# Two transformer blocks on one core: the first block's weight casts and remainders moved ahead of the convolution's taps, with four neighbouring steps

## The chip, the core and the metric

The kernel runs on one core of a Trainium2 chip, written by hand for its five engines: TensorE (PE in the rows; PEld is its weight load), VectorE (DVE), ScalarE (ACT), GpSimd (POOL) and SyncE (SP), which issues the weights' DMAs. Engines meet through semaphores only. The metric is the device time of one execution in microseconds (us).

## What is computed

Two blocks follow each other on 256 tokens of width 1024, batch 1, float32. The change lies in the mixing part of the first block, which reduces to this:

```python
h = rms_norm(x, pre_mix_norm)
proj = h @ w_in                          # att q, k, v | gdn qkv | z | a, b
o_att = softmax attention, 8 heads of 64, with relative bias
qkv = silu(causal_conv(gdn_qkv, 4 taps)) # 1536 channels
g = -exp(A_log) * softplus(a + dt_bias)  # per token and head
g_cum = cumsum(g) within chunks of 64
decay = exp(where(causal, g_cum_i - g_cum_j, -inf))
m = strict_lower(k_beta k^T * decay)     # then (I + m) is solved for u and w
o_gdn = the gated recurrence over the chunks, with q k^T * decay
x = x + rms_norm([o_att, o_gdn] @ w_out)
```

The MLP of the first block and the whole second block come behind it and are untouched.

## The kernel before, in words

Every product in float32 is made from rounded halves: a weight tile `raw` (128 x 2048) is cast to `wh` on ScalarE (function `hi`, L1152) and its remainder `raw - wh` is put into `wl` on VectorE (function `lo`, L1649). TensorE then adds three products per tile. A tile is a *unit*; units are numbered in the order of a list, PLAN, and each engine walks that list. Units 0 to 5 are the convolution's inputs (query, key and value channels, two channel groups each), 6 and 7 the gate z, 8 and 9 the attention's keys (called `qk` 0 and 1), 10 and 11 its queries (`qk` 2 and 3), 12 and 13 its values.

`raw` has 3 slots and `wh` and `wl` have 4. SyncE loads unit i into its slot when `lo(i - 3)` is done; `hi(i)` waits for the load and for TensorE to have finished unit i - 4; `lo(i)` waits for `hi(i)`; TensorE waits for `lo(i)`. On ScalarE and VectorE the call `next_unit()` issues all casts or remainders up to two units ahead of the engine's own count (AHEAD is 2).

Every engine runs its instructions in the order in which they are written. The order around the change is this.

On TensorE: units 0 to 3, the sums of the decays (L684, L685, and L689, whose result is `grow`), units 4 and 5, the two units of z (L506), the sums of squares (L658), unit 8, the turned sums `rn` and the token-major values and keys (`tm`, `kd`, transposes at L417), unit 9, then the products of keys and queries `KQ` (L752, eight banks in four pairs), units 10 and 11, and L764, which waits for VectorE's `spread`. A product goes to one of eight PSUM banks, and TensorE waits until the bank's last reader is done. Unit 4 goes to the bank of unit 2, whose reader is the scaling `cin` 2 on VectorE. The banks of `KQ` 2 and 3 were those of the second `tm` tile and of `kd`; the bank of `KQ` 5 was that of unit 9.

On VectorE, a loop over u = 0 to 5: scale the unit's output into `cin` (L1670), `next_unit()`, then six tap instructions (L1678) that add the taps 1 to 3 to the tap 0 that ScalarE has made. For u = 3 it also copies the cumulated decays (`gcum`) and prepares `kdx`, which frees a bank that z uses. For u = 5 there are eight of the sixteen differences of `dU` before the taps and eight after the loop (`differences`, one instruction for each of 16 pairs of chunk pair and head). Then come `keys(0)`, a scaling of unit 8's output that waits for that unit; the norms up to `bk`; the product of `dU` with `bk` (`db`); `kdx` and `kd`; the remainders of units 10 and 11; `keys(1)`, which waits for unit 9; a loop over the eight `KQ` banks; and, without another wait for TensorE, the steps up to `spread` (L1670).

On ScalarE, the loop over u casts ahead, makes the taps 0 (L1290) and, for u = 3, copies `grow` out of PSUM, sends it to DRAM, runs three `silu` instructions, waits for that DMA and reads the rows back, spread over all partitions, into `dU`. Behind the loop it casts units 8 and 9, then makes the squares (L1269) that TensorE's sums of squares need.

Of the kernel before, what the change touches and what calls it, by code (L numbers as in the profile page):

```python
# [189 lines left out]
def rep(a, m):  # L190
    return a.unsqueeze(1).broadcast_to([128, m, a.shape[1]])
# [10 lines left out]
def halves(a):  # L202
    return a.rearrange("p (a s) -> p a s", a=2)
# [162 lines left out]
def build(nc, A, out):  # L366
    with ExitStack() as top:
# [15 lines left out]
        def par(name):  # L383
            a, w = SM[name]
            return M.small[:, a:a + w]
# [752 lines left out]
        def scalar(e):  # L1138
# [4 lines left out]
            def hi(upto):  # L1143

                while done[0] < min(upto + 1, len(PLAN)):
                    i = done[0]
                    done[0] += 1
                    r, h = i % RR, i % HR
                    q.wait_dma(raw_in[r], 16 * (i // RR + 1))
                    if i >= HR:  # L1150
                        q.wait_ge(PE, ("unit", i - HR))
                    e.copy(M.wh[:, h, :], M.raw[:, r, :]).then_inc(q.sem, q.tick(("hi", i)))  # L1152

            def next_unit():
                hi(unit[0] + AHEAD)
                unit[0] += 1
# [102 lines left out]
            def silu_of(u):  # L1259
                q.wait_ge(DV, ("tap", 2 * u + 1, 3))  # L1260
                o = M.cout[:, 2 * u:2 * u + 2, :]
                e.activation(o, o, ACT.Silu).then_inc(q.sem, q.tick(("silu", u)))
# [9 lines left out]

            for u in range(6):
                next_unit()
                if u == 0:
                    q.wait_ge(DV, "sn0")
                    e.activation(M.sn, M.sn, ACT.Exp).then_inc(q.sem, q.tick("sn1"))
                    q.wait_ge(DV, "eb")
                    e.activation(M.eb1, M.eb1, ACT.Exp, scale=-1.0).then_inc(q.sem, q.tick("eb1"))
                    q.wait_dma(LD["small"])  # L1280
                    e.activation(M.ea, par("A_log"), ACT.Exp).then_inc(q.sem, q.tick("ea"))
                    q.wait_ge(q, "sn1")
                    e.activation(M.sn, M.sn, ACT.Ln, bias=1.0).then_inc(q.sem, q.tick("sn2"))
                if u == 4:
                    silu_of(3)
                q.wait_ge(DV, ("cin", u))
                q.wait_ge(PO, "pad")
                for i in range(2):
                    a = 2 * u + i
                    e.activation(M.cout[:, a, :], M.cin[:, a, 0:S], ACT.Copy,  # L1290
                                 scale=cw[:, a, 0:1]).then_inc(q.sem, q.tick(("tap", a, 0)))
                if u == 3:
                    q.wait_ge(PE, "grow")
                    e.copy(M.grow, bank[at["grow"]][0:16, 0:128]).then_inc(q.sem, q.tick("grow"))
                    q.wait_ge(q, "grow")
                    e.dma_start(A["gscr"], M.grow).then_inc(LD["gscr"], 16)
                    silu_of(0)
                    silu_of(1)
                    silu_of(2)
                    q.wait_dma(LD["gscr"])  # L1300
                    e.dma_start(M.dU[:], bass.AP(A["gscr"].tensor, 0, [[0, 128], [128, 16], [1, 128]])).then_inc(
                        LD["dU"], 16)
                elif u == 5:
                    silu_of(4)
# [331 lines left out]
        def vector(e):  # L1636
# [4 lines left out]
            def lo(upto):  # L1641

                while done[0] < min(upto + 1, len(PLAN)):
                    i = done[0]
                    done[0] += 1
                    r, h = i % RR, i % HR
                    q.wait_dma(raw_in[r], 16 * (i // RR + 1))
                    q.wait_ge(AC, ("hi", i))
                    e.tensor_tensor(M.wl[:, h, :], M.raw[:, r, :], M.wh[:, h, :].bitcast(F32),  # L1649
                                    ALU.subtract).then_inc(q.sem, q.tick(("lo", i)))  # L1650

            def next_unit():
                lo(unit[0] + AHEAD)
                unit[0] += 1
# [14 lines left out]
            def tt(o, a, b, op, *names):  # L1669
                return e.tensor_tensor(o, a, b, op).then_inc(q.sem, q.tick(*names))  # L1670

            def ts(o, a, s1, s2, op0, op1, *names):
                if op1 is None:
                    return e.tensor_scalar(o, a, s1, None, op0).then_inc(q.sem, q.tick(*names))
                return e.tensor_scalar(o, a, s1, s2, op0, op1).then_inc(q.sem, q.tick(*names))

            def stt(o, a, s, b, op0, op1, *names):
                return e.scalar_tensor_tensor(out=o, in0=a, scalar=s, in1=b, op0=op0,  # L1678
                                              op1=op1).then_inc(q.sem, q.tick(*names))
# [98 lines left out]
            def scaled(u):  # L1778
                q.wait_ge(PE, ("conv", u))
                q.wait_ge(AC, "rbc")  # L1780
                tt(M.cin[:, 2 * u:2 * u + 2, 3:], halves(bank[at["conv", u]][:]), rep(M.rbc, 2), ALU.mult, ("cin", u))
# [8 lines left out]
            def differences(lo_, hi_):  # L1790
                q.wait_dma(LD["dU"])
                for s in range(lo_, hi_):
                    stt(M.dU[:, s, :], M.dU[:, s, :], M.gcum[:, s:s + 1], M.cap, ALU.subtract, ALU.min, "dU")

            for u in range(6):
                if u:
                    scaled(u)
                if u < 5:
                    next_unit()
                if u == 0:  # L1800
                    q.wait_ge(AC, "eb1")
                    ts(M.eb1, M.eb1, 1.0, None, ALU.add, None, "eb2")
                    q.wait_ge(q, "eb2")
                    e.reciprocal(M.beta, M.eb1).then_inc(q.sem, q.tick("beta"))
                    q.wait_ge(AC, "sn2")
                    stt(M.sn, M.sa1, 0.0, M.sn, ALU.max, ALU.add, "sn3")
                    q.wait_ge(q, "sn3")
                    q.wait_ge(AC, "ea")
                    stt(M.graw.rearrange("p (c h) -> p c h", c=2), M.sn.rearrange("p (c h) -> p c h", c=2), -1.0,
                        rep(M.ea, 2), ALU.mult, ALU.mult, "graw")  # L1810
                elif u == 5:
                    next_unit()
                    differences(0, 8)
                    next_unit()
                for k in range(1, 4):
                    for i in range(2):
                        a = 2 * u + i
                        q.wait_ge(AC if k == 1 else q, ("tap", a, k - 1))
                        stt(M.cout[:, a, :], M.cin[:, a, k:k + S], cw[:, a, k:k + 1], M.cout[:, a, :], ALU.mult,
                            ALU.add, ("tap", a, k))  # L1820
                if u == 3:
                    q.wait_ge(PE, "sums")
                    b = at["sums"]
                    e.tensor_copy(M.gcum, bank[b][:, 0:16]).then_inc(q.sem, q.tick("gc"))
                    q.wait_ge(q, "gc")
                    tt(M.kdx, bank[b][:, 16:32], M.gcum, ALU.subtract, "kdx0")

            differences(8, 16)
            next_unit()

            def keys(u):

                q.wait_ge(PE, ("qk", u))
                tt(M.kTa[:, 2 * u:2 * u + 2, :], halves(bank[at["qk", u]][:]), rep(M.rbc, 2), ALU.mult, ("qk", u))
# [11 lines left out]
            e.reciprocal(bk, rk).then_inc(q.sem, q.tick("bk0"))  # L1846
            q.wait_ge(q, "bk0")
            tt(M.bk, M.bk, M.beta, ALU.mult, "bk")
            q.wait_ge(AC, "dexp")
            q.wait_ge(q, "bk")  # L1850
            tt(M.dU[:], M.dU[:], bc(M.bk, 128), ALU.mult, "db")
# [3 lines left out]
            q.wait_ge(PE, "kd")  # L1855
            tt(heads(M.kd), heads(bank[at["kd"]][:]), bc(M.kdx[:, 0:8], 64), ALU.mult, "kd")
            next_unit()
            next_unit()
            keys(1)

            def att_scores(h):
                nm = gs[:, 192 + 4 * (h % 4):194 + 4 * (h % 4)]
# [590 lines left out]
        for engine in (tensor, scalar, vector, gpsimd):  # L2453
            engine(Counting())
# [4 lines left out]
        block.sync(sync)  # L2459
        block.gpsimd(gpsimd)  # L2460
        block.scalar(scalar)
        block.vector(vector)
        block.tensor(tensor)

# [48 lines left out]
```

## Time and profile before

| | |
|---|---|
| median of 3 runs | 901.58 us (900.99 to 903.89) |
| the profiled execution's own time | 901.5 us |
| its span, first to last instruction | 899.3 us |
| mean granted TensorE clock | 0.997 of full speed |

The span and the own time belong to one execution; the 2.2 us between them lie outside the program's instructions. Times in the rows further down are us from the start of the span.

### The profile page before, as it was taken

The page shows a single profiled execution, that of the slowest core. Times are in us where ns is not written, and L with a number is a line of the kernel's source. Part 1 is how long each engine was busy: PE and PEld are TensorE (multiplying, and loading weights), DVE is VectorE, ACT ScalarE, POOL GpSimd, SP SyncE. Part 2 cuts the span into 40 slices and gives each one's busy share as a digit, 9 for nine tenths or more (in the row PEclk, how much of TensorE's full clock was granted, in tenths as well). Part 3 has the DMA queues.
Part 4 walks back from the last instruction along what each step waited for, and adds up shares of the span by engine and source line. Part 5 has one row for each costly group of instructions (what it writes and reads, how often), then busy time and mean ns, then how long its engine had stood idle before and what let it go on. Part 6 is the DMA issues. An engine that isn't in the chain of part 4 may idle for free.

```text
span 899.3 us, 12704 instructions
## 1 busy us (share of the span) xinstructions
PE 886.7 (99%) x5404; PEld 758.7 (84%) x5404; DVE 608.4 (68%) x734; ACT 455.8 (51%) x550; POOL 82.6 (9%) x93
## 2 busy tenths in 40 slices
PE   9999999999999999999999999999999999999997
PEld 8889788788888887888888888888888888888885
DVE  5989886776556657778858665766557566664655
ACT  6683563654445446555443355443355555444543
POOL 1001230100000000000124210110100000000000
PEclk9999999999999999999999999999999999999999
DMA  9675315156555553654564544354554356455531
GB/s 329 257 253 185 101 59 201 48 175 257 195 193 187 188 187 140 223 188 156 206 220 168 187 166 162 141 187 187 187 187 147 155 190 234 176 180 206 187 141 47
DMA packets 26264, 161.51 MB, mean 180 GB/s; under 512 B 3608, under 2 KB 4280, under 8 KB 8288
## 3 DMA queue, kind: packets, MB, share of 16 engines
q1 hardware_dynamic: 23616, 153.40, 46.7%
q0 software_dynamic: 2272, 6.24, 2.0%
q10 hardware_dynamic: 320, 1.06, 0.3%
q8 instruction: 42, 0.69, 0.3%
q14 instruction: 14, 0.11, 0.0%
HBM read 159.62 MB, written 2.64 MB: 180 GB/s over the span
## 4 chain that ended last, share of the span: by engine, by line
PE 79%; DVE 13%; ACT 3%; DMA 2%; issue 2%; SPq 1%; POOL 0%; POOLq 0%; ACTq 0%; DVEq 0%
PE banks L506 34%; PE banks L474 21%; PE banks L477 10%; DVE t_wl L1649 5%; PE banks L578 3%; PE banks L534 2%; PE banks L417 1%; DMA t_x<-in_x 1%; PE banks L775 1%; ACT t_wh L1152 1%; DVE t_xt L1670 1%; PE banks L980 1%; PE banks L1114 1%; DVE t_cout L1678 1%; PE banks L429 1%
## 5 line engine op out<-in xcount | busy, mean ns | idle before, releaser
L1649 DVE TENSOR_TENSOR t_wl<-t_raw,t_wh 128x2048 fp32r<-128x2048 f32 x136 | 312.2, 2317 | 111.2 <-ACT t_wh L1152 110.1
L474 PE MATMUL banks<-t_hx,t_wh 128*128 128x512 f32 x992 | 312.0, 396 | 0.0
L1152 ACT CAST t_wh<-t_raw 128x2048 fp32r<-128x2048 f32 x136 | 255.8, 1906 | 15.9 <-DMA t_raw<-in_W 9.4
L477 PEld LDWEIGHTS banks<-t_hx,t_wl 128*128 128x128 f32 x992 | 186.3, 188 | 43.7
L477 PE MATMUL banks<-t_hx,t_wl 128*128 128x256 f32 x992 | 194.9, 278 | 0.0
L474 PEld LDWEIGHTS banks<-t_hx,t_wh 128*128 128x128 f32 x992 | 153.4, 189 | 2.4
L506 PE MATMUL banks<-t_wh,t_hx 128*128 128x512 f32 x320 | 101.7, 394 | 0.2 <-DVE t_wl L1649 0.2
L506 PEld LDWEIGHTS banks<-t_wh,t_hx 128*128 128x128 f32 x320 | 59.5, 188 | 13.0 <-DVE t_wl L1649 0.4
L506 PE MATMUL banks<-t_wl,t_hx 128*128 128x512 f32 x160 | 61.1, 390 | 0.0
L2297 POOL TENSOR_TENSOR t_st<-t_st,t_half 128x1 f32<-128x1 f32 (+1 forms) x18 | 10.6, 589 | 433.6 <-DVE t_st L1678 425.7
L1487 ACT COPY t_hold<-banks 128x512 f32<-128x512 f32 x28 | 16.4, 584 | 65.3 <-PE banks L477 54.7
L429 PE MATMUL banks<-t_hx,t_wh 128*128 128x256 f32 x192 | 36.5, 292 | 1.9 <-DVE t_wl L1649 1.9
L1446 ACT COPY t_tail<-banks 128x512 f32<-128x512 f32 x14 | 8.2, 586 | 54.8 <-PE banks L477 54.8
L506 PEld LDWEIGHTS banks<-t_wl,t_hx 128*128 128x128 f32 x160 | 30.1, 188 | 6.1
L506 PE MATMUL banks<-t_wh,t_mh 128*128 128x512 f32 x112 | 34.6, 390 | 0.0
L506 PE MATMUL banks<-t_wl,t_mh 128*128 128x512 f32 x112 | 34.5, 389 | 0.0
L506 PE MATMUL banks<-t_wh,t_ml 128*128 128x512 f32 x112 | 34.5, 389 | 0.0
L429 PEld LDWEIGHTS banks<-t_hx,t_wh 128*128 128x128 f32 x192 | 31.0, 199 | 2.9 <-DVE t_wl L1649 2.2
L1670 DVE TENSOR_TENSOR t_rl<-banks,t_tail 128x512 f32<-128x512 f32 x14 | 9.7, 691 | 28.0 <-ACT t_tail L1446 28.0
L429 PE MATMUL banks<-t_hx,t_wl 128*128 128x256 f32 x96 | 27.8, 290 | 0.0
L2397 POOL TENSOR_SCALAR t_gt<-t_gt,t_small 128x256 f32<-128x256 f32 x16 | 14.6, 926 | 117.6 <-ACT t_gt L1556 117.6
L1613 ACT COPY t_gtail<-banks 128x512 f32<-128x512 f32 x11 | 6.4, 586 | 37.4 <-PE banks L477 37.4
(335 smaller groups left out, 1322.3 us busy)
## 6 DMA issues: line engine op xcount, KB each, us to landing
t_raw<-in_W SPq DMA_DIRECT2D x139, 1024.0 KB, 4.8
t_raw<-in_W SPq DMA_DIRECT2D x8, 256.0 KB, 6.3
t_raw<-in_W SPq DMA_DIRECT2D x4, 512.0 KB, 9.1
skew<-scr POOLq DMA_DIRECT2D x1, 1536.0 KB, 14.4
t_cout<-in_xT SPq DMA_DIRECT2D x4, 256.0 KB, 5.3
t_x<-in_x SPq DMA_DIRECT2D x2, 512.0 KB, 10.8
t_dU<-gscr ACTq DMA_DIRECT2D x1, 1024.0 KB, 7.5
t_tab<-in_tab POOLq DMA_DIRECT2D x1, 640.0 KB, 7.6
```

Source lines behind the costliest of these rows:

```text
L429: m = e.matmul(bank[b][:, c * S:c * S + S], W[w][:, h, k * 256 + c * 128:k * 256 + c * 128 + 128], H[a][:, k, :], start=k == 0 and n == 0, ...
L474: e.matmul(bank[b + c], M.wh[:, h, wk], M.hx[:, k, :, :].rearrange("p a s -> p (a s)"), start=k == 0, stop=False)
L477: m = e.matmul(bank[b + c][:, 0:S], M.wl[:, h, wk], M.hh[:, k, :], start=False, stop=k == 7)
L506: m = e.matmul(bank[outs[t][c]][:], act[a][:, ks[kk], t * 128:t * 128 + 128], W[w][:, h, kk * 512 * ncb + c * 512:kk * 512 * ncb + c * 512 ...
L534: m = e.matmul(bank[outs[t][c]][:], act[a][:, k, t * 128:t * 128 + 128], W[w][:, (i0 + u) % HR, kk * 1024 + c * 512:kk * 1024 + c * 512 + ...
L578: m = e.matmul(bank[bo][:], H[a][:, k, t * 128:t * 128 + 128], W[w][:, (i0 + k // 4) % HR, (k % 4) * 512:(k % 4) * 512 + 512], start=k == ...
L1152: e.copy(M.wh[:, h, :], M.raw[:, r, :]).then_inc(q.sem, q.tick(("hi", i)))
L1487: e.copy(halves(M.rest[:, s, :]), both(M.banks, at[tile], 1)).then_inc(q.sem, q.tick((tile, "rest")))
L1649: e.tensor_tensor(M.wl[:, h, :], M.raw[:, r, :], M.wh[:, h, :].bitcast(F32), ALU.subtract).then_inc(q.sem, q.tick(("lo", i)))
L1670: return e.tensor_tensor(o, a, b, op).then_inc(q.sem, q.tick(*names))
L2297: return e.tensor_tensor(o, a, b, op).then_inc(q.sem, q.tick(*names))
L2397: e.tensor_scalar(M.gt[:, a, :], M.gt[:, a, :], gw[:, 4 * h + a:4 * h + a + 1], None, ALU.mult).then_inc(q.sem, q.tick(("gt", h, a)))
```

## The change

Four edits, all in the order of instructions; no instruction is added or removed.

1. In the loop over u, ScalarE casts and VectorE subtracts one unit further ahead, before the taps of step u: unit 4 at u = 1, unit 5 at u = 2, unit 6 at u = 3, and units 7 and 8 before the taps of u = 4. ScalarE's cast of unit 7 stands behind the taps of u = 3.
2. ScalarE copies `grow` and sends it to DRAM at u = 2. The three `silu`, the wait for that DMA and the read into `dU` stay at u = 3, behind the cast of unit 7.
3. VectorE makes the 16 differences together, behind the loop and behind the remainder of unit 9 (before, that remainder stood behind them).
4. VectorE makes the remainder of unit 10 and then `keys(1)` right behind `bk`, ahead of `db`, `kdx` and `kd`; the remainder of unit 11 stays behind `kd`.

```diff
 # scalar
             for u in range(6):
                 next_unit()
+                hi(min(u + 3, 6) if u < 4 else 8)
...
-                if u == 3:
+                if u == 2:
                     q.wait_ge(PE, "grow")
                     e.copy(M.grow, bank[at["grow"]][0:16, 0:128]).then_inc(q.sem, q.tick("grow"))
                     q.wait_ge(q, "grow")
                     e.dma_start(A["gscr"], M.grow).then_inc(LD["gscr"], 16)
+                elif u == 3:
+                    hi(7)
                     silu_of(0)
                     silu_of(1)
                     silu_of(2)
 # vector
                 if u < 5:
                     next_unit()
+                    lo(u + 3 if u < 4 else 8)
...
                 elif u == 5:
                     next_unit()
-                    differences(0, 8)
                     next_unit()
...
-            differences(8, 16)
+            lo(9)
+            differences(0, 16)
             next_unit()
...
             tt(M.bk, M.bk, M.beta, ALU.mult, "bk")
+            next_unit()
+            keys(1)
             q.wait_ge(AC, "dexp")
             q.wait_ge(q, "bk")
             tt(M.dU[:], M.dU[:], bc(M.bk, 128), ALU.mult, "db")
...
             tt(heads(M.kd), heads(bank[at["kd"]][:]), bc(M.kdx[:, 0:8], 64), ALU.mult, "kd")
             next_unit()
-            next_unit()
-            keys(1)
```

## Rows read from the trace of the kernel before

**Rows 1.** The page, part 1: busy time, share of the span, instructions.

```profile
PE 886.7 (99%) x5404; PEld 758.7 (84%) x5404; DVE 608.4 (68%) x734; ACT 455.8 (51%) x550; POOL 82.6 (9%) x93
```

**Rows 2.** TensorE's waits over the span: us in total, times, longest.

```profile
PE banks L429 <- DVE t_wl L1649: 1.9, 1, 1.9
...
PE banks L619 <- POOL t_st L2297: 0.6, 1, 0.6
```

**Rows 3.** The chain that ended last, 30 to 100 us: start, length, what.

```profile
40.67 4.67 DMA gscr<-t_va
...
45.74 1.92 ACT t_wh L1152
...
50.10 11.18 PE banks L506 x48
...
62.28 5.95 PE banks L429 x48
...
90.34 1.24 DVE t_cin L1670
...
91.62 1.99 PE banks L764 x4
```

**Rows 4.** Timeline of TensorE: start, us, line, operation, tiles, [idle before <-releaser].

```profile
34.34 0.39 PE L689 MATMUL banks<-t_tab,t_gs 128*16 128x128 f32 x2
36.63 0.79 PE L429 MATMUL banks<-t_hx,t_wh 128*128 128x256 f32 x2 [1.90 <-DVE t_wl L1649]
...
62.21 0.51 PE L429 MATMUL banks<-t_hx,t_wh 128*128 128x256 f32 x2
...
75.66 2.00 PE L752 MATMUL banks<-t_cout 64*128 64x256 f32 x16
77.89 2.00 PE L752 MATMUL banks<-t_cout 64*128 64x256 f32 x16 [0.23 <-DVE t_kTa L1670]
```

**Rows 5.** Two stretches: us, busy us by engine, granted clock, DMA share, GB/s.

```profile
20.00:36.60 16.60, 14.09 (x112) 12.91 (x110) 13.32 (x32) 10.99 (x19) 3.30 (x5) 1.00 0.71 276
36.65:40.05 3.40, 3.40 (x16) 3.40 (x17) 3.40 (x8) 0.92 (x3) 0.00 (x0) 0.50 0.64 228
```

**Rows 6.** Timeline of VectorE, 30 to 78 us.

```profile
30.04 0.68 DVE L1670 TENSOR_TENSOR t_cin<-banks,t_rbc 128x512 f32<-128x512 f32 x1
...
33.68 0.69 DVE L1670 TENSOR_TENSOR t_cin<-banks,t_rbc 128x512 f32<-128x512 f32 x1
34.28 2.29 DVE L1649 TENSOR_TENSOR t_wl<-t_raw,t_wh 128x2048 fp32r<-128x2048 f32 x1
36.48 2.46 DVE L1678 SCALAR_TENSOR_TENSOR t_cout<-t_cin,t_small,t_cout 128x256 f32<-128x256 f32 x6
...
61.81 2.19 DVE L1678 SCALAR_TENSOR_TENSOR t_dU<-t_dU,t_gs,t_tab 128x128 f32<-128x128 f32 x8
...
69.73 2.29 DVE L1670 TENSOR_TENSOR t_dU<-t_dU,t_gs 128x2048 f32<-128x2048 f32 x1
...
72.14 0.69 DVE L1670 TENSOR_TENSOR t_tm<-banks,t_gs 128x512 f32<-128x512 f32 x1
...
77.15 0.69 DVE L1670 TENSOR_TENSOR t_kTa<-banks,t_rbc 128x512 f32<-128x512 f32 x1
77.75 0.41 DVE L1678 SCALAR_TENSOR_TENSOR t_hold<-banks,t_dU 128x256 f32<-128x256 f32 x1
```

**Rows 7.** Timeline of ScalarE, 41 to 61 us.

```profile
41.03 1.28 ACT L1262 ACT_TABLE_LOAD   x1 [0.39 <-ACT t_va L1294]
42.32 1.68 ACT L1262 ACTIVATE t_cout<-t_cout 128x512 f32<-128x512 f32 x3
...
53.06 0.91 ACT L1290 ACTIVATE t_cout<-t_cin,t_small 128x256 f32<-128x256 f32 x2 [2.28 <-DVE t_cin L1670]
...
58.51 2.00 ACT L1269 ACTIVATE t_cin<-t_cout 128x1024 f32<-128x1024 f32 x2
```

**Rows 8.** DMA issues between 36.5 and 36.8 us: size, us to landing.

```profile
t_raw<-in_W SPq DMA_DIRECT2D x1, 1024.0 KB, 8.9
```

## The prediction

> **What bounds the kernel now.** I read the busy shares first. TensorE is busy for 99% of the span [rows 1], so a gain has to come from the few places where TensorE waits, or runs at half its clock. Then TensorE's waits: the only long one is 1.9 us for unit 4's remainder [rows 2]; behind it the granted clock stands at 0.50 for 3.4 us, that is at 1.2 of 2.4 GHz, after 1.00 before [rows 5]. The reader should not book those 1.9 us and the lost clock as the gain, for the chain that ended last says what really sets the pace next: the decays' rows go to DRAM at 40.67 and take 4.67 us, ScalarE can't pass the wait for them and casts unit 6 only at 45.74, and so z starts at 50.10 [rows 3]. TensorE's late unit 4 was hidden behind that. The next place on the chain is `spread`: it ends at 90.34 + 1.24 = 91.58, and TensorE's L764, which waits for it, starts at 91.62 [rows 3]. From the first instruction of the loop over the `KQ` banks, at 77.75, VectorE needs 13.83 us to that end [rows 3, 6], and nothing in the loop or behind it waits for TensorE, whose `KQ` is written by then. So the sum needs two times in the new order: when TensorE reaches z and unit 8, and when VectorE reaches the `KQ` loop.
>
> **The casts one step ahead.** Steps on VectorE, from start to start: a scaling takes 0.60 us (33.68 to 34.28), a remainder 2.20 (34.28 to 36.48), six taps 2.46 less the 0.09 by which neighbours overlap, 2.37 [rows 6]. The order up to the scaling at 30.04 is untouched. From there: unit 4's remainder at 30.64, the taps of u = 1 at 32.84, the scaling of u = 2 at 35.21, ending at 35.89. The remainder is ready 3.7 us sooner, but unit 4 on TensorE wants the PSUM bank that this scaling reads out, so it starts at about 35.95 and not at 34.73, where the sums end (34.34 + 0.39), nor at 36.63 as before [rows 4]. The gap shrinks from 1.90 to 1.2 us. Does the clock still fall? A wait of 0.6 us left it at 1.00, one of 1.90 didn't [rows 2, 5]; 1.2 us lies half way. I take it that it holds, because the shortened gap leaves 0.7 us of matmuls in the place of idleness, and keep the fall for a rival.
>
> Units 4 and 5 at full clock take about 5.9 us each (5.95 for a unit with its last matmul, [rows 3]), together 11.8 with the overlap: TensorE is ready for z at 47.75. z needs unit 6's remainder (VectorE: scaling of u = 3 at 40.4, remainder 41.0 to 43.2) and the bank that the sums of the decays left (read by 45.9). ScalarE's cast of unit 6 now stands before the silu and ends by 39.3. Nothing is late, and z starts 2.35 us sooner.
>
> **The decays' rows.** `grow` is copied by 37 instead of 40.6; its DMA lands at 41.7 by the 4.67 of [rows 3]. ScalarE has by then: taps of u = 3 to 42.0, cast of unit 7 to 43.9 (its load is issued 3.7 us sooner too, and with the 8.9 us of [rows 8] lands at 41.8), table load 1.28 and three silu 1.68 [rows 7], so the read into `dU` is issued at 46.9, behind 45.4 before, without a wait. At 8.9 us, the slowest load of that size here, it lands at 55.8. The differences start at 59.9, so its delay costs nothing. SyncE's queue only gains: each load waits for a remainder, and those come sooner.
>
> **ScalarE becomes the next limit.** Cast of unit 8 to 49.2 (1.92 us a cast, [rows 3]); VectorE's remainder of unit 8 waits 0.4 us for it and ends at 51.4; taps, then the last scaling ends at 54.4. Then ScalarE makes its last taps (0.91), one silu (0.56), the cast of unit 9 (1.92) and the squares (2.00) [rows 3, 7], which end at 59.7. TensorE ends z at 47.75 + 11.18 = 58.9 [rows 3], and the second half of the sums of squares waits for those squares: unit 8 starts at 60.2 against 62.21 [rows 4]. The lead is 2.0 us.
>
> **The differences together.** Sixteen take 2 x 2.19 less an overlap, 4.3 us [rows 6]; with unit 9's remainder ahead of them they run from 59.9 to 64.2, against an end at 64.0 before. ScalarE's exponential and cast of unit 10 follow by 68.2 and VectorE's remainder of unit 10 by 70.4. All this lies beside TensorE's units 8 and 9. Without that cover, each 0.1 us would be paid.
>
> **The second keys' scaling.** This is where the lead goes. TensorE's work from unit 8's start to `KQ` is 75.66 - 62.21 = 13.45 us [rows 4], so `KQ` starts at 73.65, and `keys(1)`, which needs the last matmul of unit 9, can't start before 73.75. VectorE reaches it at 70.4 and stands still for 3.35 us with `db`, `kdx`, `kd`, unit 11's remainder and the `KQ` loop queued behind it. Before, `db` to `kd` and most of both remainders ran while TensorE made unit 9. Now, from 73.75: `keys(1)` 0.60, `db` with `kdx` 2.41 (69.73 to 72.14), `kd` 0.60, remainder 2.20 [rows 6]. The loop starts at 79.56 against 77.75, 1.8 us late in spite of the lead of 2.0. What the edit buys is the 0.23 us that TensorE waited for `keys(1)` at 77.89 [rows 4].
>
> TensorE meets it too: the third bank pair's partner in `KQ` 2 and 3 is read by `kd`, which ends at 73.75 + 0.60 + 2.41 + 0.69 = 77.45. After the first pair (1.0 of 2.00 us) TensorE idles from 74.7 to 77.5. From there it needs 1.0 and then what it needed between 77.89 and 91.6, 13.7 us [rows 3, 4]: it is ready for L764 at 92.2, and `spread` comes at 91.58 + 1.81 = 93.4. So L764 is 1.8 us late. But a gap of 2.8 us is longer than the one behind which the clock fell; 3.4 us at half clock [rows 5] cost up to 1.7, which uses up the 1.2 us of slack and puts L764 at up to 93.9. I take 93.6: plus 2.0 us. Bounds: plus 1.8 without the fall, plus 2.3 with all of it. TensorE and VectorE both stand behind `spread`, and I see no slack that gives the time back.
>
> The Trainium skill has two places that bear on this. "TensorE: Matmul & The Clock Gate", in "Architectural detail", says that ScalarE and VectorE queues are strictly first in, first out. By this rule `db` can't pass the waiting `keys(1)`; if it could, the lead would carry through and the time be 899.5. The same page's table under "Why this matters for your kernels" lets a gap longer than 1.90 us pass before the clock falls; by it neither gap costs any and the time is 903.3. This trace shows a fall behind 1.90 us, and the measurement decides.
>
> **The sum.** The profiled execution took 901.5 us, 2.2 more than its span; it is 0.1 under the median of 901.58, so I take it for the median. 901.5 + 2.0 = 903.5.
>
> **The rivals.**
> First, the clock falls in the first gap as well. It decides if 1.2 us of idleness behind the small matmuls of the sums are enough. Units 4 and 5 then take up to 1.7 us more, z ends at 60.6, its squares are no longer waited for, and unit 8 starts at 61.6 instead of 60.2. Everything behind is 1.4 later: 904.9, slower by 0.4%. For it: 1.90 us were enough. Against: 0.6 were not. Page "TensorE: Matmul & The Clock Gate", "What's actually happening", of the Trainium skill says that the monitor doesn't start over with a kernel, so the same gap may do it in one run and not in the next; no row here shows it.
> Second, the hold doesn't bind: unit 9 is done when VectorE asks, and the lead of 2.0 stays, 899.5. That needs unit 9 to end at 70.4, 3.3 us sooner than TensorE's own work allows; or else VectorE's other work turns out short. Little speaks for it.
> Third, nothing is seen: the lateness at `spread` is taken up in the next stage, where short steps pass between three engines, 901.5. For it: SyncE and ScalarE have slack there. Against: TensorE and VectorE are late together.
>
> **How the numbers follow.** Forecast, 903.3 to 903.9: 0.55. First rival 0.20, second 0.10, third 0.15. About 0.3%, 2.7 us, is what a measurement of this kernel can tell from no change; slower thus begins at 904.3. Slower: most of the first rival and the forecast's upper tail, 0.28. Faster, under 898.9: part of the second, 0.06. Same: 0.66. The range reaches from 900.0, between the second and the third rival, to 905.4, over the first.
>
> **What would show it.** Right: unit 4 waits about 1.2 us for `cin`, with the clock at 1.00 behind it; z starts near 47.8; unit 8 near 60.2; VectorE idles over 3 us before the second scaling of keys; TensorE idles 2 to 3 us inside `KQ`, for `kd`; L764 starts near 93.5. Wrong: another transfer or cast that stops ScalarE between 42 and 58, no idle time before `keys(1)`, or an L764 that is no later than 91.6.

## The result, and the profile after

The changed kernel takes 903.66 us (median of 10 runs, 903.17 to 904.57) against 901.25 us of the kernel before (10 runs beside it). The ratio is 1.0026, with a 95% interval of 1.0016 to 1.0036: 2.4 us slower, a loss that the interval tells from nothing, and one of the size that was forecast (2.0 us).

The profiled execution of the changed kernel has a span of 902.5 us, 3.2 more than that of before. Not all of this belongs to the change: VectorE's scaling of u = 1, ahead of everything that was moved, starts at 30.80 instead of 30.04 [rows 6], because `x` was loaded later (ScalarE's first work on it starts at 19.66 instead of 18.91). Where absolute times of two traces are compared below, such a shift is taken off (0.76 us here), which puts both on the scale of before. What is left is 2.1 us from L764 on, and still 2.1 us at L1114 in the second block (712.81 against 709.98). About 0.35 us more appear only behind it, where nothing was changed and where this execution has a wait of 0.21 us that the other lacks; I count them as chance. So the traces show a loss of 2.1 us, the medians one of 2.4 us with an interval of 1.4 to 3.2.

TensorE's waits in the changed kernel, over the span:

```profile
PE banks L752 <- DVE t_tm L1673: 2.8, 1, 2.8
PE banks L429 <- DVE t_cin L1673: 1.3, 1, 1.3
...
PE banks L658 <- ACT t_cin L1269: 0.6, 2, 0.3
```

The wait of 1.9 us for unit 4's remainder [rows 2] is one of 1.3 us for the scaling of u = 2, and a new wait stands above it: 2.8 us inside `KQ`, for the tile that `kd` writes. TensorE's timeline shows where:

```profile
36.81 0.36 PE L429 MATMUL banks<-t_hx,t_wh 128*128 128x256 f32 x1 [1.31 <-DVE t_cin L1673]
...
48.40 0.40 PE L506 MATMUL banks<-t_wh,t_hx 128*128 128x512 f32 x1
...
61.26 0.50 PE L429 MATMUL banks<-t_hx,t_wh 128*128 128x256 f32 x2
...
74.69 1.13 PE L752 MATMUL banks<-t_cout 64*128 64x256 f32 x8
78.64 4.31 PE L752 MATMUL banks<-t_cout 64*128 64x256 f32 x24 [2.82 <-DVE t_tm L1673]
...
94.50 0.68 PE L764 MATMUL banks<-t_cin,t_tab 128*128 128x512 f32 x1
```

z (L506) starts directly behind unit 5 at 48.40, or 47.64 on the scale of before, where 47.75 was worked out. Unit 8 starts at 61.26, or 60.5 on the scale of before, against 62.21 [rows 4]: the lead is there, 1.7 us. `KQ` starts at 74.69, and 4 us later TensorE is still at its first quarter. L764 starts 2.88 us later than in [rows 3], 2.12 with the shifted start taken off. VectorE's timeline has the reason:

```profile
69.39 2.29 DVE L1652 TENSOR_TENSOR t_wl<-t_raw,t_wh 128x2048 fp32r<-128x2048 f32 x1 [0.74 <-ACT t_wh L1152]
74.79 0.69 DVE L1673 TENSOR_TENSOR t_kTa<-banks,t_rbc 128x512 f32<-128x512 f32 x1 [3.11 <-PE banks L429]
75.40 2.28 DVE L1673 TENSOR_TENSOR t_dU<-t_dU,t_gs 128x2048 f32<-128x2048 f32 x1
...
77.80 0.69 DVE L1673 TENSOR_TENSOR t_tm<-banks,t_gs 128x512 f32<-128x512 f32 x1
78.41 2.28 DVE L1652 TENSOR_TENSOR t_wl<-t_raw,t_wh 128x2048 fp32r<-128x2048 f32 x1
80.61 0.42 DVE L1681 SCALAR_TENSOR_TENSOR t_hold<-banks,t_dU 128x256 f32<-128x256 f32 x1
...
93.20 1.22 DVE L1673 TENSOR_TENSOR t_cin<-t_kb,t_tab 128x1024 f32<-128x1024 f32 x1
```

The reader should follow VectorE's queue: the remainder of unit 10 ends at 71.68, then nothing for 3.11 us, because the scaling of the second keys (first row with `t_kTa`) waits for TensorE's unit 9. Only then come `db`, `kdx` and `kd`, which in [rows 6] ran from 69.73 on, while TensorE still made that unit. The `KQ` loop starts at 80.61 instead of 77.75, `spread` ends at 94.42 instead of 91.58. That is the loss, 2.1 us on the common scale.

The long gap also cost TensorE its clock, while the gap ahead of unit 4 did not, as three stretches show (us, busy us of PE, PEld, DVE, ACT and POOL, granted clock, DMA share, GB/s):

```profile
36.90:48.00 11.10, 11.10 (x93) 11.10 (x94) 11.06 (x19) 8.43 (x11) 0.00 (x0) 1.00 0.86 326
...
78.25:81.55 3.30, 2.91 (x14) 2.60 (x16) 3.30 (x5) 0.00 (x0) 0.00 (x0) 0.50 0.00 0
81.65:94.50 12.85, 12.85 (x109) 12.45 (x107) 12.68 (x22) 2.40 (x2) 1.03 (x2) 1.00 0.47 164
```

`KQ` runs on at 1.2 GHz, half the clock. It matters little: TensorE ends unit 11 just when `spread` ends, so the fall used up TensorE's slack and added less than 0.1 us.

On ScalarE one thing went otherwise than forecast:

```profile
42.62 0.34 ACTq L1304 DMA_DIRECT2D t_dU<-gscr  x1
42.69 1.89 ACT L1152 CAST t_wh<-t_raw 128x2048 fp32r<-128x2048 f32 x1
44.60 1.28 ACT L1262 ACT_TABLE_LOAD   x1
45.89 1.68 ACT L1262 ACTIVATE t_cout<-t_cout 128x512 f32<-128x512 f32 x3
48.18 1.92 ACT L1152 CAST t_wh<-t_raw 128x2048 fp32r<-128x2048 f32 x1 [0.61 <-DMA t_raw<-in_W]
```

The read into `dU` (ACTq) is written behind the cast of unit 7 and the three silu, yet it is issued at 42.62, ahead of them: as soon as the DMA of the decays' rows that it waits for had landed (issued at 37.78, 4.8 us to landing). So the sentence that every engine runs its instructions in the order in which they are written does not hold for a DMA that ScalarE's program issues. The cast of unit 8 then waits 0.61 us for its load.

### The profile page after: what moved, and what is told of

Its sections match the earlier page's. It is cut to its first block, busy times and chain, and to the rows that moved or that the text cites. A ratio compares the mean times of both kernels' runs of the same rounds, so it can differ in the third digit from the quotient of the medians.

```text
span 902.5 us, 12704 instructions
## 1 busy us (share of the span) xinstructions
PE 886.7 (98%) x5404; PEld 758.4 (84%) x5404; DVE 608.0 (67%) x734; ACT 455.6 (50%) x550; POOL 83.7 (9%) x93
## 4 chain that ended last, share of the span: by engine, by line
PE 77%; DVE 13%; ACT 5%; DMA 2%; issue 2%; SPq 1%; POOL 0%; POOLq 0%; DVEq 0%; ACTq 0%
PE banks L506 32%; PE banks L474 19%; PE banks L477 10%; DVE t_wl L1652 6%; PE banks L429 3%; PE banks L578 3%; PE banks L534 2%; ACT t_wh L1152 2%; PE banks L417 1%; DMA t_x<-in_x 1%; PE banks L775 1%; DMA t_raw<-in_W 1%; PE banks L980 1%; DVE t_cout L1681 1%; DVE t_cv L1681 1%
## 5 line engine op out<-in xcount | busy, mean ns | idle before, releaser
L506 PE MATMUL banks<-t_wh,t_hx 128*128 128x512 f32 x320 | 101.6, 394 | 0.0
L506 PEld LDWEIGHTS banks<-t_wh,t_hx 128*128 128x128 f32 x320 | 59.5, 188 | 12.5 <-issue 0.3
L506 PE MATMUL banks<-t_wl,t_hx 128*128 128x512 f32 x160 | 61.1, 390 | 0.0
L506 PEld LDWEIGHTS banks<-t_wl,t_hx 128*128 128x128 f32 x160 | 30.1, 188 | 6.1
L506 PE MATMUL banks<-t_wh,t_mh 128*128 128x512 f32 x112 | 34.6, 390 | 0.0
L506 PE MATMUL banks<-t_wl,t_mh 128*128 128x512 f32 x112 | 34.5, 389 | 0.0
L506 PE MATMUL banks<-t_wh,t_ml 128*128 128x512 f32 x112 | 34.5, 389 | 0.0
## 6 DMA issues: line engine op xcount, KB each, us to landing
t_dU<-gscr ACTq DMA_DIRECT2D x1, 1024.0 KB, 11.6
```

The lines of the kernel that those rows point to most:

```text
L506: m = e.matmul(bank[outs[t][c]][:], act[a][:, ks[kk], t * 128:t * 128 + 128], W[w][:, h, kk * 512 * ncb + c * 512:kk * 512 * ncb + c * 512 ...
```

## The experiments

The comparisons are with the kernel before, run on the same chip beside each group. Kernels that build on others are named by what they change. Where the times of two runs are subtracted, the medians are; the ratio compares each run with the kernel before beside it.

**Is it the second keys?** First the fourth edit undone, then that edit alone.

```diff
             tt(M.bk, M.bk, M.beta, ALU.mult, "bk")
-            next_unit()
-            keys(1)
...
             next_unit()
+            next_unit()
+            keys(1)
```

> The changed kernel with the fourth edit undone (remainder of unit 10 and second keys' scaling back behind the decays' product and kd). If the hold of VectorE at the second keys' scaling is the whole loss: VectorE makes the decays' product, kd and both remainders while TensorE makes unit 9, no wait of over 1 us before that scaling, TensorE's wait inside KQ at most 1 us, and spread 1.2 us sooner than in the kernel before: 900.1, ratio 0.9985. If the casts one step ahead are themselves what costs (loads that collide, ScalarE held up): still about 903.5, ratio 1.0025.

Measured: 899.5 us, ratio 0.9979 (0.9970 to 0.9987). VectorE's timeline of this run:

```profile
67.20 2.29 DVE L1673 TENSOR_TENSOR t_dU<-t_dU,t_gs 128x2048 f32<-128x2048 f32 x1
69.41 0.17 DVE L1673 TENSOR_TENSOR t_gs<-t_gs 128x16 f32<-128x16 f32 x1
69.61 0.69 DVE L1673 TENSOR_TENSOR t_tm<-banks,t_gs 128x512 f32<-128x512 f32 x1
70.22 4.48 DVE L1652 TENSOR_TENSOR t_wl<-t_raw,t_wh 128x2048 fp32r<-128x2048 f32 x2
74.62 0.68 DVE L1673 TENSOR_TENSOR t_kTa<-banks,t_rbc 128x512 f32<-128x512 f32 x1
75.22 0.41 DVE L1681 SCALAR_TENSOR_TENSOR t_hold<-banks,t_dU 128x256 f32<-128x256 f32 x1
```

No row has idle time before it: the same instructions fill the time of unit 9, and the loop starts at 75.22, or 75.91 on the scale of before, 1.8 us sooner than there. `spread` is 1.9 us sooner, where 1.2 was expected. Three of the four edits make the kernel 2.1 us faster; the fourth turns that into a loss of 2.4.

> The kernel before with the fourth edit alone. If the hold is the loss, it costs more here, where there is no lead of 2 us to pay for it: the KQ loop starts 3.8 us later than in the kernel before, L764 3.8 to 4.3 us later, 905.1 to 905.6, ratio 1.0043 to 1.0048, and TensorE waits about 2.8 us for kd inside KQ. If the loss comes from the casts: no change, or the 0.2 us that TensorE waited for the second keys.

The edit is the other half of the diff, put into the kernel before. Measured: 905.66 us, ratio 1.0047 (1.0035 to 1.0060). Alone the fourth edit costs 4.1 us, as was worked out. TensorE's waits:

```profile
PE banks L752 <- DVE t_tm L1670: 2.8, 1, 2.8
PE banks L506 <- DVE t_wl L1649: 2.1, 2, 1.8
```

The second row bears on the reading of the kernel before. In this run the clock stood at 1.00 behind the gap of 1.88 us ahead of unit 4. Its stretch, and then the start of z in this run and in the kernel before (both traces are on the same scale):

```profile
36.65:40.05 3.40, 3.40 (x28) 3.40 (x29) 3.40 (x8) 0.92 (x3) 0.00 (x0) 1.00 0.61 234
...
50.20 0.50 PE L506 MATMUL banks<-t_wh,t_hx 128*128 128x512 f32 x1 [1.79 <-DVE t_wl L1649]
...
50.10 0.50 PE L506 MATMUL banks<-t_wh,t_hx 128*128 128x512 f32 x1 [0.19 <-DVE t_wl L1649]
```

TensorE was ready for z at 48.41, 1.5 us sooner than the 49.91 of the kernel before, and stood 1.8 us waiting for unit 6's remainder. z started at 50.20, with the fallen clock at 50.10. So the lost clock ahead of unit 4 was indeed hidden: in this stage TensorE could be later by nearly those 1.8 us without z being later.

**Does TensorE's wait for `kd` count by itself?**

```diff
             tt(M.bk, M.bk, M.beta, ALU.mult, "bk")
-            next_unit()
-            keys(1)
-            q.wait_ge(AC, "dexp")
             q.wait_ge(q, "bk")
-            tt(M.dU[:], M.dU[:], bc(M.bk, 128), ALU.mult, "db")
...
             tt(heads(M.kd), heads(bank[at["kd"]][:]), bc(M.kdx[:, 0:8], 64), ALU.mult, "kd")
             next_unit()
+            keys(1)
+            q.wait_ge(AC, "dexp")
+            tt(M.dU[:], M.dU[:], bc(M.bk, 128), ALU.mult, "db")
+            next_unit()
```

> The changed kernel with kdx and kd ahead of the remainder of unit 10 and the second keys' scaling; the decays' product and the remainder of unit 11 stay behind it. TensorE's bank is then free when it reaches KQ 2 and 3. If VectorE's lateness sets the end and TensorE's wait for kd adds only what the fallen clock costs: spread 0.6 to 0.8 us sooner than in the changed kernel, 902.5 to 902.8, ratio 1.0014 to 1.0017. If TensorE's wait of 2.8 us for kd is the cause by itself: 2 us sooner or more, about 901, ratio 1.000.

Measured: 902.7 us, ratio 1.0013 (1.0004 to 1.0022). TensorE no longer waits inside `KQ`; it waits behind it, for the first bank that the late loop frees:

```profile
PE banks L429 <- DVE t_dU L1673: 2.2, 1, 2.2
```

The clock stood at 0.50 there too (80.00 to 83.30). The loop starts 0.9 us sooner than in the changed kernel on the scale of before, which is about the time of `kdx` and `kd` on VectorE, and the median is 1.0 us lower. So TensorE's wait for `kd` is not the cause by itself: without it VectorE's lateness remains, and TensorE idles for that at another place.

**Can the hold be filled the other way round?** `db`, `kdx`, `kd` and unit 10's remainder before the second keys, the loop right behind them, unit 11's remainder behind the loop and unit 12's behind `spread`.

```diff
             tt(M.bk, M.bk, M.beta, ALU.mult, "bk")
-            next_unit()
-            keys(1)
...
             tt(heads(M.kd), heads(bank[at["kd"]][:]), bc(M.kdx[:, 0:8], 64), ALU.mult, "kd")
             next_unit()
+            keys(1)
...
                ALU.mult, "spread")
             next_unit()
+            next_unit()
```

> The changed kernel, with the decays' product, kdx, kd and the remainder of unit 10 before the second keys' scaling, the KQ loop right behind it, the remainder of unit 11 behind the loop, and that of unit 12 behind spread. If the hold is the loss and the lead of 2 us is real: VectorE waits under 1 us for unit 9, the loop starts at about 74.4 on the scale of the kernel before, TensorE is the later of the two at L764 and keeps the lead: 899.3, ratio 0.998. If the next stage takes all leads back: 901.3, ratio 1.000.

Measured: 900.61 us, ratio 0.9987 (0.9978 to 0.9996): faster than before, but 1.1 us behind the plain order, and not what was forecast. TensorE's waits, and below them three rows of VectorE's timeline, say why:

```profile
PE banks L775 <- DVE t_xt L1673: 1.3, 1, 1.3
PE banks L429 <- DVE t_cin L1673: 1.3, 1, 1.3
...
74.32 0.69 DVE L1673 TENSOR_TENSOR t_kTa<-banks,t_rbc 128x512 f32<-128x512 f32 x1 [0.74 <-PE banks L429]
75.38 0.42 DVE L1681 SCALAR_TENSOR_TENSOR t_hold<-banks,t_dU 128x256 f32<-128x256 f32 x1 [0.36 <-PE banks L752]
...
89.11 4.49 DVE L1652 TENSOR_TENSOR t_wl<-t_raw,t_wh 128x2048 fp32r<-128x2048 f32 x2
```

L764 no longer waits for `spread`, but two remainders now stand between `spread` and a later product of VectorE that TensorE needs (`t_xt`, L775). VectorE had idled 0.74 us for the second keys and 0.36 us ahead of the loop, together the 1.1 us that are missing. With the plain order it is idle for only 0.40 us between the first keys' scaling and that product. My reading is that VectorE has next to no time to spare there: putting off work moves the wait, and an idle moment is lost.

**What limits the lead?** The next four take the run with the fourth edit undone as their base, or, the last of them, the kernel before.

```diff
                 at_unit(("conv", u), DV, ("cin", u),
-                        mid=(None, None, roots_and_gates, None, None, None)[u])
+                        mid=(None, None, roots_and_gates, None, None, None)[u], **({"to": 2} if u == 4 else {}))
+                turn[0] += u == 4
```

> The best run so far (the changed kernel with the fourth edit undone, 0.9979 of before) with unit 4 sent to a free bank, so that it needn't wait for the scaling of u = 2. If ScalarE's squares are the next limit, as the prediction has it: unit 4's gap of 1.3 us goes, z ends 1.3 us sooner, and TensorE's sums of squares wait 1.3 us longer (0.5 becomes 1.8 us); the time stays at 0.998. If TensorE's own order sets the pace there: 1.3 us faster, 0.9965.

Measured: 899.59 us, ratio 0.998 (0.9971 to 0.9990), the base's time. Unit 4's gap is gone and the time stands before the sums of squares (TensorE's timeline):

```profile
58.45 0.64 PE L658 MATMUL banks<-t_cin,t_tab 128*32 128x256 f32 x8 [1.79 <-ACT t_cin L1270]
```

```diff
             next_unit()
-            next_unit()
             squares(0)
             squares(1)
+            next_unit()
...
-            lo(9)
             differences(0, 16)
+            lo(9)
```

> The same best run with ScalarE's squares ahead of the cast of unit 9 (and VectorE's 16 differences ahead of that unit's remainder). If the squares are the limit: TensorE's wait of 0.5 us at the sums of squares goes and unit 8 starts 0.5 us sooner, 0.9973; no more, because z's end is next. If the later remainder of unit 9 or the decays' exponential matter: no gain or a loss.

Measured: 898.95 us, ratio 0.9971 (0.9960 to 0.9983). TensorE's wait at L658 is gone, and the step is of the size expected, though the interval overlaps the base's.

> Both: unit 4 in a free bank and the squares ahead of the cast of unit 9. If the two limits stand one behind the other, neither edit gives much alone and both together give 1.5 to 1.8 us on the best run so far: 0.9960 to 0.9963, about 898. If VectorE's work from unit 8 on is the real limit, the lead ends at the second keys and the time stays at 0.998.

Measured: 898.06 us, ratio 0.9966 (0.9953 to 0.9978). Together the two edits give 1.4 us on the base by the medians and 1.2 by the ratios, under the 1.5 to 1.8 that were expected, but more than either alone.

```diff
-                if u == 3:
+                if u == 2:
                     q.wait_ge(PE, "grow")
...
                     e.dma_start(A["gscr"], M.grow).then_inc(LD["gscr"], 16)
+                elif u == 3:
                     silu_of(0)
```

> The kernel before with the second edit alone (the decays' rows copied and sent one step sooner). The chain of waits of the kernel before put z's start on that DMA. If so, the wait of 1.7 us of ScalarE ahead of the cast of unit 6 goes; z then starts when TensorE ends unit 5, which is 0.2 to 2 us sooner depending on whether the clock falls behind the gap of 1.9 us, or when the remainder of unit 6 is made: 0.998 to 1.000. If the DMA is not what holds z: 1.000 with z at the same time.

Measured: 900.3 us, ratio 0.9983 (0.9974 to 0.9992). The second edit alone brings 1.1 us on the 901.42 beside it. After nearly the same gap, 1.89 us, ahead of unit 4 the clock did fall here, and z began directly behind unit 5, without waiting for a remainder, 0.4 us sooner on the scale of before (49.26 plus 0.48, against 50.10):

```profile
36.55:39.85 3.30, 3.30 (x17) 3.30 (x17) 3.30 (x7) 1.49 (x3) 0.00 (x0) 0.50 0.68 256
...
49.26 0.40 PE L506 MATMUL banks<-t_wh,t_hx 128*128 128x512 f32 x1
```

So the copy of the decays' rows was what held z, as the chain of waits said, and without it the fallen clock is no longer hidden. The second keys' scaling is 0.5 us sooner on that scale; the rest of the 1.1 us doesn't show there.

**The early read.**

```diff
                 if u == 4:
+                    q.wait_dma(LD["gscr"])
+                    e.dma_start(M.dU[:], bass.AP(A["gscr"].tensor, 0, [[0, 128], [128, 16], [1, 128]])).then_inc(
+                        LD["dU"], 16)
                     silu_of(3)
...
                     silu_of(2)
-                    q.wait_dma(LD["gscr"])
-                    e.dma_start(M.dU[:], bass.AP(A["gscr"].tensor, 0, [[0, 128], [128, 16], [1, 128]])).then_inc(
-                        LD["dU"], 16)
```

> The best order of the second edit's read, on the changed kernel with the fourth edit undone: the read of the decays' rows into dU is written behind the cast of unit 8 instead of ahead of it, so that ScalarE's sequencer can't issue it while the engine is still on earlier work. If that early read is what made unit 8's load late: the load lands sooner, ScalarE's wait of 0.5 us ahead of the cast of unit 8 goes, the squares and unit 8's start come up to 0.5 us sooner: 0.9973 to 0.9979. If the load is slowed by the decays' other copy (the relative bias rows, 1.5 MB) alone: no change in that wait.

Measured: 899.2 us, ratio 0.9969 (0.9958 to 0.9980). ScalarE's timeline:

```profile
45.33 1.67 ACT L1262 ACTIVATE t_cout<-t_cout 128x512 f32<-128x512 f32 x3
46.64 0.34 ACTq L1287 DMA_DIRECT2D t_dU<-gscr  x1
46.91 1.90 ACT L1152 CAST t_wh<-t_raw 128x2048 fp32r<-128x2048 f32 x1
```

The cast of unit 8 follows the silu directly. That unit's load took 8.3 us instead of 9.2, and ScalarE's wait of 0.5 us for it is gone; against the base the time itself can't be told apart. The read goes out while the silu still run, but 4.5 us later than in the base on the scale of before: just when unit 8's load has landed (issued at about 38.3), for which the cast ahead of the read has to wait. In all seven profiled runs that cast one step ahead and read early, the cast of unit 8 waited 0.31 to 0.78 us for its load; in this run and the next it did not. One thing in this trace has nothing to do with the edit: the granted clock was 0.51 from 25.0 to 28.5 us, so TensorE reached unit 4 later, and the 1.3 us gap ahead of it is missing.

> All that helped together: casts ahead, the fourth edit undone, unit 4 in a free bank, squares ahead of the cast of unit 9, the read of the decays' rows behind the cast of unit 8. Against the run with both (0.9966) only the read differs; if unit 8's load was held by it, up to 0.4 us more, 0.9962 to 0.9966.

Measured: 897.67 us, ratio 0.9948 (0.9934 to 0.9963). The best version, 4.3 us faster than the kernel before beside it and about 6 us faster than the changed one by the medians. Against the run with both edits it is 0.4 us faster, as expected; the ratio fell further than that, and below the 0.9962 to 0.9966 expected, because the kernel before was slower beside this group (901.99 against 901.42). The intervals of the two overlap, so what the read adds isn't settled.

## Why the prediction was right

The forecast of 903.5 holds for 903.66. That the two lie within 0.2 us is in part luck: the step was 2.4 us instead of 2.0, from a base that was 0.25 us lower. The smallest change that a measurement can tell was also put too high, at 2.7 us; the interval here is 0.9 us to either side. The steps can be taken in turn.

**The hidden wait.** Right: z was held by the decays' rows, not by unit 4. The second edit alone moved z, and a run in which the clock didn't fall ahead of unit 4 started z at the same time as one in which it did.

**Unit 4's bank.** Right: a gap of about 1.2 us for the scaling was forecast, 1.31 measured, with the clock at full speed behind it (1.00 from 36.90 to 48.00 in the changed kernel). So the first rival, a second fall, didn't come. The clock held in all five profiled runs with a gap of 1.30 or 1.31 us. But the rival was nearer than the argument against it, that 1.2 us lies half way between a wait that was harmless and one that was not: behind gaps of 1.88 to 1.90 us the clock fell in two runs and held in a third, and in the run with the late read it fell with no wait longer than 0.77 us in the 10 us before. So this step came out right with some luck. The Trainium skill's sentence on a monitor that doesn't start over with a kernel ("TensorE: Matmul & The Clock Gate", "What's actually happening") agrees with this.

**ScalarE as the next limit.** Right in kind: sending unit 4 elsewhere changed nothing until the squares came sooner. In size the lead at unit 8 was 1.7 us instead of 2.0. The largest single part of this is the cast of unit 8, which waited 0.61 us for its load; the sum had left about 0.4 us behind the silu, and so the cast ended 0.14 us later than worked out (50.10, or 49.34 on the scale of before, against 49.2). The rest adds up in small steps behind it. What was wrong is the read into `dU`: on the scale of before it was issued at 41.86, 5.0 us sooner than the 46.9 that I worked out, and the run with the late read shows that the wait goes with it. A stop of ScalarE between 42 and 58 us was one of the signs of being wrong; it came, and was small.

**The hold.** Right: 3.35 us forecast, 3.11 measured. The `KQ` loop was to start 1.8 us late and was 2.1 us late on the common scale, the 0.3 us being the smaller lead. Undone, the loss becomes a gain of 2.1 us, the second rival's 899.5; alone, the edit costs 4.1 us. The rule that VectorE's queue is first in, first out (the Trainium skill, "TensorE: Matmul & The Clock Gate", "Architectural detail: the array is 16× 32×32, not 1× 128×128") agrees with these two runs.

**The clock inside `KQ`.** The fall came where it was forecast. Its price was taken as 0.2 us and was under 0.1: TensorE's unit 11 and VectorE's `spread` ended together. This error and the smaller lead nearly cancel: L764 was forecast at 93.6 and came at 93.74 on the scale of before.

**Nothing gives it back.** Right: the lateness at L764, 2.1 us, is still 2.1 us at L1114 in the second block, and within 0.3 of the difference of the medians, so the third rival fell.

Open is how much of the last gain, 0.4 us by the medians, belongs to the read.

## What to carry to other kernels

Before an instruction that waits is moved ahead in a queue, list what then stands behind it and what that work ran beside: a wait of 0.23 us was removed here for one of 3.1. A lead on one engine is worth only what the next engine in line can take up, so follow it to the first wait that did not move. Take a long wait of TensorE for a gain only after the chain of waits shows that nothing later would have stopped it anyway.

## What the runs showed of the hardware that wasn't expected

A DMA that ScalarE's program issues need not wait for the computing instructions ahead of it: the read into `dU`, written behind a cast and three silu, went out at 42.62 while the engine was still at the taps before them, and landed after 11.6 us; unit 8's load, issued at 38.9, took 9.3 us beside it, and 8.3 in the run where the read came later. A wait that is not yet met does hold such an issue: in that run the read, written behind the cast of unit 8, went out only at 46.64, when the load that this cast needs had landed.

The clock's fall isn't fixed by the length of a gap: 1.88 us ahead of unit 4 left the clock at 1.00 in one run, 1.89 and 1.90 us took it to 0.50 in two others. Nor was a short gap always harmless: in the run with the late read it was 0.51 from 25.0 to 28.5 us, with 0.77 us (L619, at 22.43) as the longest wait of TensorE in the 10 us before, while waits of 0.74 or 0.75 us at the same line left it at 1.00 in four other runs.
